# 128x128 state steps, selection rounds among the softmax steps, reordered first transfers and a new last norm in a hybrid decoder step

## The reference, cut to what matters

```python
def decoder_layer(x, ...):
    n = rmsnorm(x, norm1)
    c_rw, c_att, c_gate = split(n @ w_in, ...)       # 3392, 2640, 4096 columns
    o_rw  = rwkv7_mix(c_rw, ...)
    o_att = attend(q, k, v, qi, ki, wi)              # dsa_prompt / dsa_sample
    merged = sigmoid(g_rw) * (o_rw @ p_rw) + sigmoid(g_att) * (o_att @ p_att)
    h = x + merged @ w_o
    return h + conv_glu(rmsnorm(h, norm2), w_up, w_down)   # d_ff 5632

def step(S, r, w, k, v, a, b):                       # rwkv7_mix, each token and head
    sa = einsum('hij,hj->hi', S, a)
    S = S * w[:, None, :] + sa[..., None] * b[:, None, :] + v[..., None] * k[:, None, :]
    return S, einsum('hij,hj->hi', S, r)

def index_select(qi, wi, ki, qpos, topk):            # prompt: topk 64
    score = einsum('bqh,bqhl->bql', wi, relu(einsum('bqhd,bld->bqhl', qi, ki)))
    return top_k(where(causal, score, -inf), topk)

y = rmsnorm(h, norm_f)                               # after the layer: y = h * rsqrt(mean(h*h) + 1e-6) * g
```

## Time and profile before

| | |
|---|---|
| median of the runs | 1784.6 us |
| profiled execution, its time | 1784.55 us |
| its span in the trace | 1783.0 us |
| TensorE busy | 1762.4 us (99%), 16500 matmuls |
| weight loads busy | 1704.9 us (96%) |
| VectorE busy | 1119.2 us (63%) |
| ScalarE busy | 759.8 us (43%) |
| GpSimd busy | 53.6 us (3%) |
| weight splits on ScalarE, L587 | 468.8 us, 1789 ns each |
| weight splits on VectorE, L567 | 503.8 us, 2117 ns each |
| moved | 283.46 MB, mean 159 GB/s |
| granted TensorE clock | 0.998 of full |

### The profile page before, as it was taken

The page is one execution under the profiler, slowest core; times in us unless marked ns, Lnnn a source line. Parts: engine busy times, 40 slices in busy tenths (PEclk is TensorE's granted clock), DMA queues, the critical chain, the costliest instruction groups (busy, mean ns, idle before and its releaser), DMA issues.

```text
span 1783.0 us, 40707 instructions
## 1 busy us (share of the span) xinstructions
PE 1762.4 (99%) x16500; PEld 1704.9 (96%) x16500; DVE 1119.2 (63%) x1995; ACT 759.8 (43%) x1059; POOL 53.6 (3%) x103
## 2 busy tenths in 40 slices
PE   9999999999999999999999999999999999999997
PEld 8999899988888888999999999999999999999996
DVE  7764954667777777765566666666666665444444
ACT  6456444555555554433443333333333333333332
POOL 2500000000000000000000000000000000000000
PEclk9999999999999999999999999999999999999999
DMA  7644344433332333644454444444444444555553
GB/s 279 227 162 163 130 160 152 155 114 107 108 107 104 111 108 113 222 166 151 174 219 165 165 165 165 165 165 165 165 165 165 165 165 162 175 169 174 169 170 132
DMA packets 51696, 283.46 MB, mean 159 GB/s; under 512 B 7248, under 2 KB 11856, under 8 KB 25776
## 3 DMA queue, kind: packets, MB, share of 16 engines
q1 hardware_dynamic: 43632, 260.35, 41.7%
q10 hardware_dynamic: 3744, 12.56, 2.0%
q0 software_dynamic: 4256, 9.65, 1.8%
HBM read 274.26 MB, written 8.27 MB: 158 GB/s over the span
## 4 chain that ended last, share of the span: by engine, by line
PE 95%; DVE 3%; DMA 1%; ACT 0%; issue 0%; DVEq 0%; SPq 0%
PE bank L621 30%; PE bank L623 28%; PE bank L622 28%; PE bank L945 1%; PE bank L985 1%; DVE w_lo L567 1%; DVE scores L1919 1%; PE bank L852 0%; PE bank L905 0%; DVE max L1886 0%; DMA x_raw<-in_x 0%; PE bank L800 0%; PE bank L817 0%; PE bank L1046 0%; PE bank L642 0%
## 5 line engine op out<-in xcount | busy, mean ns | idle before, releaser
L621 PE MATMUL bank<-x_split,w_lo 128*128 128x288 f32 x2880 | 873.2, 303 | 3.3 <-DVE w_lo L567 2.1
L622 PE MATMUL bank<-x_split,w_hi 128*128 128x288 f32 x2880 | 849.5, 295 | 0.0
L623 PE MATMUL bank<-x_split,w_hi 128*128 128x288 f32 x2880 | 847.0, 294 | 0.0
L587 ACT ACTIVATE w_hi<-w_raw 128x2048 fp32r<-128x2048 f32 (+1 forms) x262 | 468.8, 1789 | 590.9 <-PE bank L623 578.7
L567 DVE TENSOR_TENSOR w_lo<-w_raw,w_hi 128x2048 fp32r<-128x2048 f32 (+1 forms) x238 | 503.8, 2117 | 283.7 <-ACT w_hi L587 283.4
L621 PEld LDWEIGHTS bank<-x_split,w_lo 128*128 128x128 f32 x2880 | 540.2, 188 | 20.3 <-issue 9.6
L622 PEld LDWEIGHTS bank<-x_split,w_hi 128*128 128x128 f32 x2880 | 541.0, 188 | 1.8 <-issue 0.7
L623 PEld LDWEIGHTS bank<-x_split,w_hi 128*128 128x128 f32 x2880 | 542.2, 188 | 0.0
L621 PE MATMUL bank<-act_split,w_lo 128*128 128x288 f32 x704 | 208.5, 296 | 0.0
L622 PE MATMUL bank<-act_split,w_hi 128*128 128x288 f32 x704 | 207.7, 295 | 0.0
L623 PE MATMUL bank<-act_split,w_hi 128*128 128x288 f32 x704 | 207.0, 294 | 0.0
(11 more groups left out here) (390 smaller groups left out, 1537.9 us busy)
## 6 DMA issues: line engine op xcount, KB each, us to landing
w_raw<-in_w_up SPq DMA_DIRECT2D x88, 1024.0 KB, 4.8
w_raw<-in_w_in SPq DMA_DIRECT2D x47, 1024.0 KB, 4.9
w_raw<-in_w_down SPq DMA_DIRECT2D x64, 704.0 KB, 4.0
w_raw<-in_w_gate SPq DMA_DIRECT2D x32, 1024.0 KB, 4.9
w_raw<-in_w_p SPq DMA_DIRECT2D x16, 1024.0 KB, 4.8
w_raw<-in_w_o SPq DMA_DIRECT2D x16, 1024.0 KB, 4.8
h<-in_x ACTq DMA_DIRECT2D x1, 2304.0 KB, 10.3
h_spill<-h ACTq DMA_DIRECT2D x1, 2304.0 KB, 9.6
```

What stands on the lines that cost most here:

```text
L587: actv(WHI[:, slot, 0:kt], WRAW[:, slot, 0:kt], ACT.Copy).then_inc(sem("w_hi"), 3 if isinstance(n, int) and n == 2 else 1)
L621: mm(out, wl, hi, start=first and k == ks[0], stop=False, skip_group_check=True)
L622: mm(out, w, lo, start=False, stop=False, skip_group_check=True)
L623: ins = mm(out, w, hi, start=False, stop=last and k == ks[-1], skip_group_check=True)
```

## The change

The diff has these parts.

- **First transfers.** The norm gains move from SP to the head of ScalarE's queue. x 12-16 moves behind weight 2, the main constants behind weight 3. The pair parameters and mix factors move behind the attention constants on ScalarE's queue.
- **Selection and fills.** The late tile's eight rounds leave `select` and stand in three groups: three after the normalisation of the first softmax step, two before the `streamed` call of the second (step 1), three and the mask after the normalisation of step 1. `streamed(FILL_TOPK)` is then a single call. FILL_TOPK_S goes from 25 to 33, FILL_TOPK from 30 to 12, FILL_SAMPLE from 14 to 16, FILL_SOFTMAX from 14 to 15.
- **Pairs.** The maps of the state become block matrices of 128x128 (MTB) with one head in each diagonal block, zero elsewhere (two memsets once). The state before each chunk is laid out likewise (STB, on VectorE, `state_blocks`). A step of the state loop is then one 128x128 product with 64 columns for both heads for the state, and one for the output of the step before; the last output product follows the last two blocks. `settle` goes. On VectorE the state copy comes ahead of the mixing of the next pair.
- **The end.** The sums are formed with tokens on the partitions: 2-column products of the sum of squares with ones, three token tiles. Root and reciprocal then work on 6 columns. Three diagonal matrices times the matrix of ones spread the factor in PSUM, where the five products of y_out read it. Y_PARTS are 2, 3, 4, 4, 3 tiles instead of 4, 4, 4, 2, 2.

```diff
@@ -194,13 +194,13 @@
...
 O_QUARTERS = (8, 12, 0, 4)
-Y_PARTS = (slice(0, 4), slice(4, 8), slice(8, 12), slice(12, 14), slice(14, 16))
+Y_PARTS = (slice(0, 2), slice(2, 5), slice(5, 9), slice(9, 13), slice(13, 16))
 LATE_CACHE_GROUP = 9
...
 FILL_MIX, FILL_LORA, FILL_FIRST, FILL_DECAY, FILL_BONUS = 14, 14, 10, 4, 8
-FILL_ROPE, FILL_REQUESTS, FILL_TOPK_S, FILL_TOPK, FILL_SAMPLE = 12, 2, 25, 30, 14
+FILL_ROPE, FILL_REQUESTS, FILL_TOPK_S, FILL_TOPK, FILL_SAMPLE = 12, 2, 33, 12, 16
 FILL_DOTS = (8, 7) + (8,) * 4
-FILL_SCORES, FILL_SOFTMAX, FILL_P_T, FILL_PV = 8, 14, 5, 4
+FILL_SCORES, FILL_SOFTMAX, FILL_P_T, FILL_PV = 8, 15, 5, 4
 SPLIT_LAG = 5
@@ -321,8 +321,8 @@
...
     QZ = m("q_grouped", [P, KVH, 4, AH, DS])
+    ACC = m("scores", [P, 2, SEQ])
     sel_at = m.at
-    ACC = m("scores", [P, 2, SEQ])
     ACS = m("scores_s", [NS, KEYS_S])
@@ -371,7 +371,7 @@
...
     m = region(inv_at + size_of([P, 4, CH]))
-    MT = m("chunk_map", [P, 4, CH])
+    m.at += size_of([P, 4, CH])
     QT = m("read_map", [P, 4, CH])
@@ -390,6 +390,9 @@
...
     LO = m("l_off", [P, 2, 2 * BL])
+    MTB = m("chunk_map", [P, NCH - 1, P])
+    STB = region(r0 + size_of([P, 2, DEC]))("state_blocks", [P, 2, P])
+    assert size_of([P, 2, DEC]) + size_of([P, 2, P]) <= size_of([P, 3, TE])
     MLS = region(vv_at)("m_low_s", [NS, 2, NS])
@@ -415,13 +418,15 @@
...
     HRSTD = m("h_rstd", [P, N])
+    FROOT = m("f_root", [P, 3, 2])
+    FDIAG = m("f_diag", [P, 3, P])
+    EPSC = m("rms_eps", [P, 1])
...
     FSQ = m("f_squares", [P, 2, N])
-    FRSTD = m("f_rstd", [P, N])
@@ -480,8 +485,6 @@
...
         def _(sp):
-            sp.dma_start(NORMS[:], a["norms"]).then_inc(sem("norms_in"), 16)
             def load_x(t0, t1, landed):
@@ -492,13 +495,14 @@
...
             load_x(8, 12, "x_in2")
-            load_x(12, 16, "x_in3")
...
                 if isinstance(n, int) and n == 2:
+                    load_x(12, 16, "x_in3")
+                if isinstance(n, int) and n == 3:
                     sp.dma_start(MC[:], a["main_c"]).then_inc(sem("main_c_in"), 16)
@@ -1084,22 +1088,21 @@
...
                 ins.then_inc(sem("state_s_mm"), 1)
+                def both_heads(banks, c, lhs, rhs):
+                    tt, par = divmod(c, 2)
+                    return mm(BK[banks[par]][:, tt * CH:(tt + 1) * CH], lhs, rhs, start=False, stop=False, skip_group_check=True)
                 for c in range(1, NCH):
-                    tt, par = divmod(c, 2)
                     fill(2)
+                    if c > 1:
+                        pe.wait_ge(sem("read"), v * 4 - 4 + c)
+                        both_heads(read, c - 1, STB[:, c % 2, :], QT[:, c - 1, :])
                     pe.wait_ge(sem("state"), v * 4 - 4 + c)
                     pe.wait_ge(sem("map"), v)
-                    settle(pe)
-                    for e, h in enumerate(halves):
-                        ins = grown(grow, 0, tt, MT[h, c, :], ST[h, c - 1, :], e, par)
-                    ins.then_inc(sem("state_mm"), 1)
-                    if c == 1:
-                        pe.wait_ge(sem("read"), v)
-                        settle(pe)
-                    for e, h in enumerate(halves):
-                        ins = grown(read, 0, tt, ST[h, c - 1, :], QT[h, c, :], e, par)
-                ins.then_inc(sem("y_mm"), 1)
+                    both_heads(grow, c, MTB[:, c - 1, :], ST[:, c - 1, :]).then_inc(sem("state_mm"), 1)
                 fill(2)
+                pe.wait_ge(sem("read"), v * 4)
+                both_heads(read, NCH - 1, STB[:, 0, :], QT[:, NCH - 1, :]).then_inc(sem("y_mm"), 1)
                 if not last:
@@ -1211,18 +1214,30 @@
...
                 down_units(g)
-            last_sum(2, FSUM, FSQ)
+            pe.wait_ge(sem("norm_sq_used"), KT * 2 + KT - 1)
+            for tt, t0 in enumerate(TOKEN_TILES):
+                mm(BK[2][:, 2 * tt:2 * tt + 2], FSUM[:, t0:t0 + P], mean_ones[:, 0:2], start=tt == 0, stop=False,
+                   skip_group_check=True)
+            pe.wait_ge(sem("norm_sq"), KT * 3)
+            for tt, t0 in enumerate(TOKEN_TILES):
+                ins = mm(BK[2][:, 2 * tt:2 * tt + 2], FSQ[:, (KT - 1) % 2, t0:t0 + P], mean_ones[:, 0:2], start=False,
+                         stop=tt == 2, skip_group_check=True)
+            ins.then_inc(sem("norm_sq_used"), 1)
+            for tt, t0 in enumerate(TOKEN_TILES):
+                pe.wait_ge(sem("norm_ms"), 3 + tt)
+                done = tt * P - t0
+                ins = mm(BK[3][:, t0 + done:t0 + P], mean_ones, FDIAG[:, tt, done:P], start=tt == 0, stop=tt == 2,
+                         skip_group_check=True)
+            ins.then_inc(sem("norm_sq_used"), 1)
...
         def _(act):
+            act.dma_start(NORMS[:], a["norms"]).then_inc(sem("norms_in"), 16)
             act.dma_start(WRAW[:, 0, 0:4, :].rearrange("p k c -> p (k c)"),
...
                           a["w_in"][0][:, 4 * P:8 * P]).then_inc(sem("w_second_in"), 16)
-            for dst, src in ((PRM_ALL, "pair_params"), (LMU, "lora_mu")):
-                act.dma_start(dst[:], a[src]).then_inc(sem("params_in"), 16)
             def first_hi(t0, t1, landed):
@@ -1264,6 +1279,8 @@
...
             act.dma_start(AC[:], a["att_c"]).then_inc(sem("att_c_lora_in"), 16)
+            for dst, src in ((PRM_ALL, "pair_params"), (LMU, "lora_mu")):
+                act.dma_start(dst[:], a[src]).then_inc(sem("params_in"), 16)
             actv(ROOT[:, 0:1], MEANS[:, 0:1], ACT.Sqrt)
@@ -1663,7 +1680,8 @@
...
             down_units(KT // 2 - 1, 2 * DU - 2)
-            norm_root(2, FRSTD)
+            act.wait_ge(sem("norm_sq_used"), KT * 3)
+            actv(FROOT[:].rearrange("p t x -> p (t x)"), BK[2][:, 0:6], ACT.Sqrt, bias=EPSC[:]).then_inc(sem("norm_rms"), 1)
             for i, k in enumerate(Y_PARTS):
@@ -1928,9 +1946,14 @@
...
                     eight_best(early, TOPK_P - 8 * heads[1])
-            st.done(marks_to_bias(early, BIASP[:, 0, 0:P], causal[0]))
-            select(ACC[:, 1, :], TOPK_P, BIASP[:, 1, :], causal[1], FILL_TOPK).then_inc(sem("bias_ready"), 1)
+            marks_to_bias(early, BIASP[:, 0, 0:P], causal[0]).then_inc(sem("bias_ready"), 1)
             dve.wait_ge(sem("bias_ready"), 1)
+            streamed(FILL_TOPK)
+            late = ACC[:, 1, :]
+            def late_rounds(r0, r1):
+                for r in range(r0, r1):
+                    eight_best(late, TOPK_P - 8 * r)
@@ -1949,6 +1972,8 @@
...
                     V.tensor_scalar(PROB[:, 0:2 * P], PROB[:, 0:2 * P], ST8[:, 8:9], None, ALU.mult).then_inc(sem("prob"), 1)
+                    if which == 0:
+                        late_rounds(0, 3)
                     streamed(FILL_SCORES + FILL_SOFTMAX)
@@ -1960,12 +1985,17 @@
...
                 V.tensor_reduce(ST8[:, 0:4], probs, AX.X, ALU.max, negate=True).then_inc(sem("s_max"), 1)
+                if n == 1:
+                    late_rounds(3, 5)
                 streamed(FILL_P_T + (FILL_PV if n == 1 else 0))
...
                 ins.then_inc(sem("prob"), 1)
+                if n == 1:
+                    late_rounds(5, 8)
+                    st.done(marks_to_bias(late, BIASP[:, 1, :], causal[1]))
                 streamed(FILL_SCORES + FILL_SOFTMAX)
@@ -2182,27 +2212,41 @@
...
+                def state_blocks(c):
+                    tt, par = divmod(c, 2)
+                    for e, h in enumerate(halves):
+                        ins = V.tensor_scalar(STB[h, c % 2, e * HD:(e + 1) * HD], BK[6 + par][h, tt * CH:(tt + 1) * CH],
+                                              PC[h, c:c + 1], None, ALU.mult)
+                    ins.then_inc(sem("read"), 1)
                 def state(c):
...
                 state(0)
-                V.tensor_tensor(MT[:, 1::2, :], grid(7, P, 2), spread(eye_ch, 1, [P, 2, CH]), ALU.add)
-                V.tensor_tensor(MT[:, 2, :], BK[6][:, P + CH:2 * P], eye_ch, ALU.add).then_inc(sem("map"), 1)
+                for e, h in enumerate(halves):
+                    V.tensor_tensor(MTB[h, 0::2, e * HD:(e + 1) * HD], BK[7][h, P:2 * P].rearrange("p (u f) -> p u f", u=2),
+                                    spread(eye_ch[h], 1, [CH, 2, CH]), ALU.add)
+                for e, h in enumerate(halves):
+                    ins = V.tensor_tensor(MTB[h, 1, e * HD:(e + 1) * HD], BK[6][h, P + CH:2 * P], eye_ch[h], ALU.add)
+                ins.then_inc(sem("map"), 1)
                 rv = AR[:, 1, :].rearrange("p (c f) -> p c f", f=CH)
...
                 V.tensor_tensor(QT[:, 2, :], BK[4][:, P + CH:2 * P], rv[:, 2, :], ALU.add).then_inc(sem("read"), 1)
+                state_blocks(0)
                 for c in range(1, NCH):
+                    dve.wait_ge(sem("state_mm"), v * 3 - 3 + c)
+                    state(c)
+                    if c + 1 < NCH:
+                        state_blocks(c)
                     if c == 1 and not last:
...
                         mix_prev(it + 1, 0)
-                    dve.wait_ge(sem("state_mm"), v * 3 - 3 + c)
-                    state(c)
```

(11 more changed lines are left out.)

## The result

The changed kernel takes 1796.95 us (median, 1796.77 to 1797.31), against 1784.6 us for the kernel before (four runs of each): ratio 1.0068, interval 1.0051 to 1.0086. It is 12.3 us slower, 9.4 us above the forecast of 1787.6 and outside the range. The profiled spans are 1795.7 and 1783.0 us, so 12.7 us are to be explained. TensorE's timeline cuts them up. For a stage I take the start of the same matmul in both kernels.

A forecast was written before the change was run, and what follows sets the result against it. TensorE was taken to pace everything. Opening -1.75, selection and softmax +8.3, pairs -1.9 and tail -1.6 summed to +3.05, so 1784.55 + 3.05 = 1787.6 us; range 1780.5 to 1792 (forecast's own 1785.5 to 1790, chance 0.60).

The forecast's parts named there:

- the gain beside them: Selection: waits for units 30, 31 and 32 go, 2.9 us gained, plus 0.3 of slack found elsewhere.
- The counts and the waits: Selection and softmax: block counts miss split marks, so TensorE gets new waits of 11.0 us in all.
- The term of +8.3: Selection and softmax: waits of 11.0 us and five restarts of 0.1, minus 2.9 and 0.3; bounds +5 and +10.
- Against: at 1774 ... it was still full for most of the two us: Argument against rival A: at the kernel's end, TensorE idle since 1770.92 us, the clock was still mostly full at 1774.
- rival A: Selection: clock falls in the waits of 3.6 and 4.0, some 2.7 us lost each; one 1790, both 1793; chance 0.10.
- VectorE ends the mixing just as they come: Pairs: VectorE's mixing ends as TensorE's results come, so the decay product moves 0.29 us per pair, seven times -2.0.
- rival D: Pairs: VectorE's extra 1.5 us per pair delays the decay product 0.5 us in seven pairs, +3.5, total 1793; chance 0.08.
- Unit 2 then lands at about 16.9: Opening: with x behind them, unit 2's weights come 1.4 us earlier, within a term of -1.75 us.
- I take 0 for it: Opening: ScalarE's first weight issue slides 0.4 us behind the norms, costed at 0 since the first matmul needs x too.
- TensorE's w_lo wait is gone: Opening, sign named in advance: TensorE's wait of 1.4 us for unit 2's split disappears.
- Tail: Last norm and stores: output products start 1.2 us earlier, smaller first store part; -1.6 us, bounds -0.8 and -2.2.

The follow-up runs named there:

- e5: The changed kernel with the lag of 5 (once 2) blocks taken as 0 in the softmax steps' calls, so splits go ahead of rounds and normalisations: 1781.31 us.
- e6: The changed kernel with products of the matrix of ones (13 and 15) on TensorE ahead of its waits for units 33 and 35: 1794.01 us.
- e1: The kernel before with only the selection part of the change (late tile's rounds in the softmax steps, new fill counts): 1797.49 us.
- e8: The changed kernel with the norm gains issued behind the first two weight parts on ScalarE's queue: 1799.63 us.
- e7: The changed kernel with the sample states' two additions ahead of VectorE's last state copy and the mixing of r behind the state loop: 1791.15 us.
- e2: The kernel before with only the 128x128 state steps of the pairs: 1783.95 us.
- e13: e10 with the last x part (12-16) issued behind unit 3's weights instead of unit 2's: 1780.58 us (one run).
- e9: The changed kernel with the two groups of three rounds put behind the call that places the split, counts and marks unchanged: 1785.34 us.
- e10: The changed kernel with the repairs of e5 and e7 together: 1776.16 us.

## Why the prediction was wrong, point by point

The profile came 9.7 us above the forecast of its span: 4.2 for the clock, 3.5 in the pairs, 1.3 in the opening, 0.6 in the waits and the gain beside them, 0.1 in the rest.

**The counts and the waits: right; the gain beside them mis-sized.** Forecast were waits of 3.6, 4.0, 1.5, 1.6 and 0.3 us at units 33, 35, 40, 44 and the first pair's square. The gaps in TensorE's timeline, less the usual pitch of 0.13, are 3.5, 3.9, 1.6, 1.7 and 0.4. The gain was put too high: the old waits of the earlier trace rows are 2.1 us, and the 2.9 in the sum puts 0.8 for three restarts on top, where the sum charges the new waits 0.1 for each. With 0.3 of slack that makes 3.2; e5, with no new wait left, gained 2.3. The term of +8.3 measured +8.9.

**"Against: at 1774 ... it was still full for most of the two us": this step failed.** I had the danger as rival A, with its price, and gave it 0.10. The clock fell at both long waits, and the sum had nothing for it where it cost 4.2 us. The earlier trace rows did show an idle TensorE losing the clock, and late: 0.86 over two microseconds means that it fell at about 1775.4, some 4.5 us after TensorE's last product at 1770.92. I took that one row as a reason against waits of 3.6 and 4.0. It was no bound. In the changed kernel the clock fell 2.4 us after the end of the last product ahead of the first wait (238.73 to 241.1), and at the ends of the other fifteen profiles it fell at most 2.5 us after TensorE's last product. e6 shows that idleness does it: with the gap filled, no fall. Rival A's price, 2.7 us each, fits the first spell (2.6); the second was shorter (1.6). How the 2.7 came from its rows isn't worked out there, so the fit is partly luck. The Trainium skill ("TensorE: Matmul & The Clock Gate", the section "HAM oscillation — how this bites in real kernels") says that an array that waits between bursts of matmuls starts the next burst at the slow clock. The traces agree for both waits of the changed kernel (0.50), but not for the first wait of e1 and e8 (1.00).

**Pairs, "VectorE ends the mixing just as they come": this step failed, by a mis-sized term.** TensorE's side was right: a step takes 1.24 us, two blocks and 0.44. I put VectorE's added work at 1.5 us per pair. Three state_blocks of 0.57 and 0.5 more for the maps are 2.2, for splitting by heads saves nothing: two products of 64x64 take 0.57 us together, one of 128x64 takes 0.28. VectorE's timeline in the third pair shows the state copies at 492.64 and 494.11 starting only when the mixing ahead of them is done:

```profile
490.48 0.57 DVE L2218 TENSOR_SCALAR state_blocks<-bank,chunk_decay 64x64 f32<-64x64 f32 x2
491.16 0.28 DVE L2224 TENSOR_SCALAR state<-bank,chunk_decay 128x64 f32<-128x64 f32 x1
491.36 0.57 DVE L2218 TENSOR_SCALAR state_blocks<-bank,chunk_decay 64x64 f32<-64x64 f32 x2
491.96 0.48 DVE L2062 SCALAR_TENSOR_TENSOR rkv<-cols,pair_params,rkv 128x256 f32<-128x256 f32 x1
...
494.11 0.28 DVE L2224 TENSOR_SCALAR state<-bank,chunk_decay 128x64 f32<-128x64 f32 x1
494.31 0.74 DVE L2253 TENSOR_TENSOR state_s<-state_s,bank 128x256 f32<-128x256 f32 x2
```

and the decay product behind it on TensorE:

```profile
494.29 0.33 PE L1093 MATMUL bank<-read_map,state_blocks 128*128 128x64 f32 x2
495.20 0.93 PE L856 MATMUL bank<-lora,cols 128*128 128x128 f32 x6 [0.58 <-DVE state_s L2253]
```

This is rival D's mechanism, and e7 confirms it. Its price was too high. A pair takes 45.13 us against 45.00 before, so the seven cost +0.8 (e2) where the forecast had -2.0 and rival D +3.5: the shorter TensorE steps paid most of it. The rest of the measured +1.6 is no part of rival D. The changed kernel's first pair has an "issue" stall and took 1.7 us longer than e2's, and its last pair, without the stall that the kernel before has there, took 1.0 less than before.

**Opening, "Unit 2 then lands at about 16.9": this step failed.** Its conversion started at 18.29, not near 17. SP issued the transfer at 11.41 before and at 11.38 after, so nothing of the 1.4 us could come from its issue; and the displaced x, issued 0.4 us behind it, travelled beside it: its packets start at 15.4 us in the trace, those of the weights run on until 17.2. In e13, without it, the weights came sooner. "I take 0 for it" of ScalarE's slid issue failed too: first weights 1.5 us later, first matmul 1.0 later, and the clock fell in the opening as well (0.72 over 8 to 14 us). "TensorE's w_lo wait is gone", a sign named in advance, came true without the gain that it was to show. Of the 1.75 us 0.45 came.

**Tail: right in size,** -1.5 against -1.6, of which 1.3 lie behind the last w_down product and 0.2 in the long stretch before it. The output products start 1.1 us sooner (forecast 1.2).

**The range.** Both A and D came in part. The forecast plus both in full is 1787.6 + 5.4 + 5.4 = 1798.4, near the measured 1796.95, though partly by luck: A came to 4.2 and D's mechanism to 2.8, and the rest is the opening and the stalls. Each stood alone in my list at 0.10 and 0.08, as if one excluded the other. They stand in different stretches, and a range with the top at 1792 had no room for two.

## What to carry to other kernels

Where engines place shared work by counts in fixed programs, work out for each mark which side of it the count falls on: four missed marks, by 5, 5, 1 and 2 blocks, were the 15.6 us between e5 and the changed kernel. Give a TensorE wait as long as those here (3.4 and 3.8 us) its own price and, with a real chance, that of a slow spell behind it (1.6 to 2.6 us each). One row of a falling clock is no bound for when it falls. When a step moves from TensorE to half-height operations of VectorE, count each at its full duration, and let what TensorE waits for go first.

## What the runs showed of the hardware

- Four kernels (the changed one, e1, e7, e8) have the same two long waits, 3.4 and 3.8 us, with nothing in them. At the first the granted clock fell to 0.50 in the changed kernel and e7 and stayed at 1.00 in e1 and e8; at the second it fell in all four. A slow spell went on for 3.3 to 5.9 us with TensorE working all the time: from 242.1 to 248.0 in the changed kernel, from 262.2 to 267.9 in e1. In the opening it fell to 0.50 too in the changed kernel, where TensorE had been idle for 2.1 us ahead of its first product, and stayed at 1.00 in e9 with 2.0.
- Transfers issued 0.4 us apart on one queue overlapped: 1 MB took 7.0 us (e10) beside 576 KB and 5.0 us without it, issued 0.95 us later (e13).
- 24 KB issued at 1.92 us behind two weight parts and three larger transfers landed 7 us later; issued first it took 3.3.
- TensorE's stalls marked "issue", 1.1 to 1.7 us, stood in the last pair of all four profiles with the old state steps and of one in twelve with the new ones, and in the first pair of two and of six. They move single profiles by as much as the small parts of this change, and why they come is open.
